# The first norm of a two-layer backbone, made feature block by feature block

## What is computed

```python
sc = jax.nn.silu(c);  sc_ctx = jax.nn.silu(c_ctx)
for i in range(DEPTH):
    sh1, sc1, g1, sh2, sc2, g2 = split(sc @ ada_w[i] + ada_b[i], 6)        # context: the same with sc_ctx
    h  = rmsnorm(x, norm1_w[i]) * (1 + sc1) + sh1                          # rmsnorm: x * rsqrt(mean(x*x) + eps) * w
    hc = rmsnorm(ctx, norm1_w[i]) * (1 + csc1) + csh1
    y, yc = retention(h, hc, ...) if i % 2 == 0 else neighbourhood_attention(h, hc, ...)
    x = x + g1 * y;  x = x + g2 * conv_ffn(rmsnorm(x, norm2_w[i]) * (1 + sc2) + sh2)
    ...                                                                     # the context likewise, in layer 0
return rmsnorm(x, final_norm_w)

# retention: q, k, v, g = split(h @ w_in); axial rope on latent q, k; forward and backward decay per head;
# out = (silu(g) * rmsnorm_per_head(o)) @ w_out
```

## Time and profile before

| what | us |
|---|---|
| median of 3 runs | 2104.57 |
| the runs | 2098.45, 2104.57, 2106.68 |
| the profiled execution's own time | 2100.11 |
| its span in the trace | 2098.2 |
| TensorE busy in it | 1994.6 |
| VectorE busy | 1336.1 |
| ScalarE busy | 749.5 |

### The profile page before, as it was taken

How to read it: one execution, slowest core, us unless ns; L and a number is a source line. 1 busy time by engine, 2 the same in 40 slices (tenths; PEclk the granted TensorE clock), 3 DMA queues, 4 the chain that set the end, 5 groups by cost and what they waited for, 6 DMA issues and landing times.

```text
span 2098.2 us, 30012 instructions
## 1 busy us (share of the span) xinstructions
PE 1994.6 (95%) x10500; PEld 1702.0 (81%) x10500; DVE 1336.1 (64%) x2241; ACT 749.5 (36%) x1274; POOL 97.4 (5%) x162
## 2 busy tenths in 40 slices
PE   5989999999999989999999999799999789999997
PEld 5778888888888868888888888688888668888885
DVE  5665735635745677766664567777877557557476
ACT  3333223313313343412331233456556335324242
POOL 0000000000000000000000000211111000000000
PEclk9999999999999989999999999899999899999998
DMA  7221221221221112233224324211111212222222
GB/s 278 71 90 61 100 71 61 82 91 61 79 93 61 61 41 100 92 128 120 90 90 132 108 95 152 102 46 41 55 45 35 81 61 100 100 97 93 97 93 101
DMA packets 50762, 186.40 MB, mean 89 GB/s; under 512 B 5569, under 2 KB 5569, under 8 KB 50561
## 3 DMA queue, kind: packets, MB, share of 16 engines
q1 hardware_dynamic: 37248, 136.73, 18.9%
q0 software_dynamic: 13440, 48.63, 6.9%
HBM read 181.15 MB, written 4.19 MB: 88 GB/s over the span
## 4 chain that ended last, share of the span: by engine, by line
PE 84%; DVE 7%; issue 4%; ACT 3%; DMA 1%; DVEq 0%; SPq 0%; ACTq 0%
PE acc L383 58%; PE o_ps L469 4%; PE o_ps L500 3%; PE acc L469 3%; PE acc L588 3%; PE o_ps L631 2%; PE acc L646 2%; PE acc L487 2%; PE acc L434 2%; PE o_ps L646 2%; DVE pt_lo L1548 1%; DMA x<-in_x_in_dram 1%; PE acc L621 1%; PE o_ps L420 1%; ACT w_hi L779 1%
## 5 line engine op out<-in xcount | busy, mean ns | idle before, releaser
L779 ACT ACTIVATE w_hi<-raw 128x1024 fp32r<-128x1024 f32 x232 | 245.1, 1057 | 615.3 <-PE acc L383 498.2
L1125 DVE TENSOR_TENSOR w_lo<-raw,w_hi 128x1024 fp32r<-128x1024 f32 x232 | 284.0, 1224 | 272.6 <-ACT w_hi L779 271.1
L383 PE MATMUL acc<-h_hi,w_hi 128*128 128x512 f32 x1520 | 434.6, 349 | 4.6 <-DVE w_lo L1125 3.4
L383 PE MATMUL acc<-h_lo,w_hi 128*128 128x512 f32 x1520 | 434.4, 349 | 0.0
L383 PE MATMUL acc<-h_hi,w_lo 128*128 128x512 f32 x1520 | 434.3, 349 | 0.0
L383 PEld LDWEIGHTS acc<-h_hi,w_hi 128*128 128x128 f32 x1520 | 244.0, 188 | 45.7 <-ACT u L942 4.2
L383 PEld LDWEIGHTS acc<-h_hi,w_lo 128*128 128x128 f32 x1520 | 243.9, 188 | 39.3
L383 PEld LDWEIGHTS acc<-h_lo,w_hi 128*128 128x128 f32 x1520 | 243.2, 188 | 38.9
L1253 DVE SCALAR_TENSOR_TENSOR x<-acc,mod,x 128x512 f32<-128x512 f32 (+3 forms) x136 | 81.9, 636 | 144.9 <-PE acc L383 136.0
L383 PE MATMUL acc<-act_hi,w_lo 128*128 128x512 f32 (+1 forms) x396 | 119.7, 356 | 0.0
L383 PE MATMUL acc<-act_lo,w_hi 128*128 128x512 f32 (+1 forms) x396 | 119.6, 356 | 0.0
(11 more groups left out here) (224 smaller groups left out, 3536.9 us busy)
## 6 DMA issues: line engine op xcount, KB each, us to landing
raw<-in_weights_dram SPq DMA_DIRECT2D x232, 512.0 KB, 3.3
ada_raw<-in_ada_dram POOLq DMA_DIRECT2D x80, 512.0 KB, 3.5
ada_start<-in_ada_first_dram SPq DMA_DIRECT2D x4, 2048.0 KB, 22.4
x<-in_x_in_dram SPq DMA_DIRECT2D x1, 3072.0 KB, 23.5
park_dram<-x POOLq DMA_DIRECT2D x1, 2048.0 KB, 8.1
rel<-in_bias_dram POOLq DMA_DIRECT2D x16, 128.0 KB, 2.4
out_dram<-x SPq DMA_DIRECT2D x8, 256.0 KB, 2.1
x<-park_dram POOLq DMA_DIRECT2D x1, 1536.0 KB, 9.1
```

The source lines that it names most:

```text
L383: mm = nc.tensor.matmul(tile[:, c0:c0 + cn], wt[:, b * P:(b + 1) * P], mv[:, n, c0:c0 + cn], start=(n == 0 and m == 0), stop=(n == last an ...
L779: nc.scalar.activation(w_hi[i][:, :], raw[i][:, :], ACT.Copy).then_inc(hi_split, 1)
L1125: nc.vector.tensor_tensor(w_lo[i][:, :], raw[i][:, :], w_hi[i][:, :].bitcast(F32), ALU.subtract)\
```

## The change

- `x` is loaded right behind the constants, in 4 pieces of two feature blocks, each with a semaphore of its own; `squares` waits for each piece. The rows of conditioning come behind it.
- The modulation weights come in 8 pieces of 1 MB, one for each feature block: its scale weights for DVE and its shift weights, laid out for TensorE in blocks 1, 2, 4, 6, 7 (`PE_SHIFTS`) and for DVE in blocks 0, 3, 5. The two first weight chunks stand between them. POOL's first `ada_raw` waits until the last scale row is made.
- TensorE makes `token_sums` and `spread_roots` first, then the shift rows of blocks 1 and 2, and those of 4, 6 and 7 between the values' products of blocks 1 and 2, 3 and 4, and 4 and 5.
- ACT copies the spread roots to `ss`. DVE goes block by block: the scale row, the shift row (its own, or one small addition to TensorE's), `x * root` in one instruction for all tokens, then `h_lo` of the block before. ACT makes `x * root * a + shift` in float32 and then `h_hi`, so `h_lo` is a plain difference.
- In head 0 the decay tables and the first later row (`ada_step(0)`) stand ahead of the keys instead of behind them, and ACT's gate waits until the last query is in halves.

```diff
 PARTS = ((0, LAT, 0), (LAT, CTX, 1))
+PE_SHIFTS = (1, 2, 4, 6, 7)
...
-                ada_start = [sb(f"ada_start{i}", [P, 4, D], stack=part) for i in range(4)]
+                ada_start = [sb(f"ada_start{k}", [P, 2, D], stack=part) for k in range(KC)]
...
         spread = o_ps[:, 0:2, :].rearrange("p a t -> p (a t)")
+        shifts = [o_ps[:, n % 2, 2 * n:2 * n + 2] for n in range(len(PE_SHIFTS))]
...
             sp.dma_start(small[:, :], small_in).then_inc(const_in, 16)
+            for i in range(4):
+                sp.dma_start(x[:, 2 * i:2 * i + 2, :], x_in[:, 2 * i:2 * i + 2, :]).then_inc(x_loaded[i], 16)
             for c in range(2):
                 sp.dma_start(silu_rows[:, c, :], cond_rows[c, :].partition_broadcast(P)).then_inc(rows_in, 16)
-            for i in (2, 0, 1, 3):
-                if i == 1:
-                    sp.dma_start(x[:, :, :], x_in).then_inc(x_loaded, 16)
-                sp.dma_start(ada_start[i][:, :, :], ada_first[4 * i:4 * i + 4, :, :].rearrange("a p n -> p a n"))\
-                  .then_inc(ada_start_in[i], 16)
-            sp.dma_start(raw[0][:, :], weights[0, :, :]).then_inc(raw_in[0], 16)
-            sp.dma_start(raw[1][:, :], weights[1, :, :]).then_inc(raw_in[1], 16)
+            for k in range(KC):
+                sp.dma_start(ada_start[k][:, :, :], ada_first[2 * k:2 * k + 2, :, :].rearrange("a p n -> p a n"))\
+                  .then_inc(ada_start_in[k], 16)
+                if k in (0, 2):
+                    sp.dma_start(raw[k // 2][:, :], weights[k // 2, :, :]).then_inc(raw_in[k // 2], 16)
...
         def _(pool):
-            pool.dma_start(ada_raw[:, :], ada[0, :, :]).then_inc(ada_in, 16)
             nc.gpsimd.memset(ones[:, :], 1.0).then_inc(set_up, 1)
             nc.gpsimd.iota(dist[:, :], pattern=[[1, 896]], base=-384, channel_multiplier=-1,
                            allow_small_or_imprecise_dtypes=True).then_inc(set_up, 1)
+            pool.wait_ge(start_rows, 1)
+            pool.dma_start(ada_raw[:, :], ada[0, :, :]).then_inc(ada_in, 16)
...
+            def start():
+                pe.wait_ge(set_up, 1)
+                token_sums(KC, TOK)
                 spread_roots(PARTS)
+                pe.wait_ge(cond_done, 1)
+                shift_row(1)
+                shift_row(2)
+            def shift_row(k):
+                n = PE_SHIFTS.index(k)
+                pe.wait_ge(ada_start_in[k], 16)
+                if n == 0:
+                    pe.wait_ge(spread_copied, 1)
+                elif n > 1:
+                    pe.wait_ge(shift_taken, n - 1)
+                for j in range(KC):
+                    mm = nc.tensor.matmul(shifts[n], ada_start[k][:, 1, j * P:(j + 1) * P], silu_c[:, j, :],
+                                          start=(j == 0), stop=(j == KC - 1))
+                mm.then_inc(shift_made, 1)
...
                                 mm.then_inc(full, 1)
+                        if first and k == 4:
+                            shift_row(PE_SHIFTS[4])
                     if s < 3:
                         mm.then_inc(v_used, 1)
+                    if first and s < 2:
+                        shift_row(PE_SHIFTS[2 + s])
...
                 return i, after
-            def squares(src, n, width):
+            def squares(src, n, width, loaded=None):
                 for k in range(n):
+                    if loaded is not None and k % 2 == 0:
+                        act.wait_ge(loaded[k // 2], 16)
...
+            def start_norm():
+                act.wait_ge(spread_done, 1)
+                nc.scalar.activation(ss[:, :], spread[:, 0:TOK], ACT.Copy).then_inc(spread_copied, 1)
+                nc.scalar.activation(logs[:, :, 0:2], cols["dlog"].rearrange("p (h c) -> p h c", c=2), ACT.Exp)\
+                  .then_inc(logs_done, 1)
+                split()
+                for k in range(KC):
+                    act.wait_ge(norm_t, normed.up())
+                    if k >= 2:
+                        act.wait_ge(h_lo_done, k - 1)
+                    for c0, cn, c in PARTS:
+                        ins = nc.scalar.activation(S[k % 2][:, c0:c0 + cn], S[2 + k % 2][:, c0:c0 + cn], ACT.Identity,
+                                                   scale=norm_a[:, k, c:c + 1], bias=mod[:, 0, k, c:c + 1])
+                    ins.then_inc(h_made, 1)
+                    act.wait_ge(h_made, k + 1)
+                    nc.scalar.activation(h_hi[:, k, :], S[k % 2][:, 0:TOK], ACT.Copy).then_inc(h_hi_done, 1)
+                    if k == 1:
+                        split()
+                    elif k in (3, 5, 7):
+                        value_split()
...
             def head_front(first):
                 if first:
-                    value_split()
-                    value_split()
                     take_values(True)
                     split()
+                    decay_tables()
                 for j in range(4):
                     key_hi(j)
+                if not first:
+                    decay_tables()
+                    for _ in range(OUT_SLOTS):
+                        wait_full()
+                        wait_full()
+                        split()
...
                 if first:
+                    act.wait_ge(qk_lo_done, 4)
                     gate(0, *wait_at(0))
...
             act.wait_ge(const_in, 16)
             nc.scalar.activation(silu_c[:, :, :], cond, ACT.Silu).then_inc(cond_done, 1)
-            nc.scalar.activation(logs[:, :, 0:2], cols["dlog"].rearrange("p (h c) -> p h c", c=2), ACT.Exp)\
-              .then_inc(cond_done, 1)
+            squares(x, KC, TOK, x_loaded)
             act.wait_ge(rows_in, 32)
-            nc.scalar.activation(silu_rows[:, :, :], silu_rows[:, :, :], ACT.Silu).then_inc(cond_done, 1)
-            A.next_at(1, counted=False)
-            act.wait_ge(x_loaded, 16)
-            squares(x, KC, TOK)
+            nc.scalar.activation(silu_rows[:, :, :], silu_rows[:, :, :], ACT.Silu).then_inc(rows_done, 1)
             act.wait_ge(set_up, 1)
             root(D, TOK)
-            for _ in range(2):
-                split()
-            norm(0, 0, PARTS, rooted=True, between=value_split)
+            start_norm()
...
+            def start_norm():
+                own_shift = lambda k: mod[:, 0, k, :]
+                def row(k, r, made):
+                    place = ada_start[k][:, r, :]
+                    step(nc.vector.tensor_tensor_reduce(ada_raw[:, :], place, silu_rows[:, 1, :], 1.0, 0.0, ALU.mult,
+                                                        ALU.add, mod_new[:, made, 1:2]))
                     step(nc.vector.tensor_tensor_reduce(place, place, silu_rows[:, 0, :], 1.0, 0.0, ALU.mult, ALU.add,
+                                                        mod_new[:, made, 0:1]))
+                def scale(k):
+                    dve.wait_ge(ada_start_in[k], 16)
+                    row(k, 0, k)
+                    made = nc.vector.tensor_scalar(norm_a[:, k, :], mod_new[:, k, :], lift[:, k:k + 1], norm_w[:, 0, k:k + 1],
+                                                   ALU.add, ALU.mult)
+                    if k == KC - 1:
+                        made.then_inc(start_rows, 1)
+                def shift(k):
+                    if k in PE_SHIFTS:
+                        n = PE_SHIFTS.index(k)
+                        dve.wait_ge(shift_made, n + 1)
+                        nc.vector.tensor_scalar(own_shift(k), shifts[n], ada_b[:, 0, k:k + 1], None, ALU.add)\
+                          .then_inc(shift_taken, 1)
+                    else:
+                        made = (k + KC // 2) % KC
+                        row(k, 1, made)
+                        nc.vector.tensor_scalar(own_shift(k), mod_new[:, made, :], ada_b[:, 0, k:k + 1], None, ALU.add)
+                def rooted_x(k):
+                    nc.vector.tensor_tensor(S[2 + k % 2][:, 0:TOK], x[:, k, :], ss[:, :], ALU.mult).then_inc(norm_t, 1)
+                def low(k):
+                    dve.wait_ge(h_hi_done, h_hi_made.up())
+                    nc.vector.tensor_tensor(h_lo[:, k, :], S[k % 2][:, 0:TOK], h_hi[:, k, :].bitcast(F32), ALU.subtract)\
+                      .then_inc(h_lo_done, 1)
+                step(nc.vector.tensor_scalar(lift[:, :], ada_b[:, 0, KC:2 * KC], 1.0, None, ALU.add))
+                add_squares(KC, TOK)
+                dve.wait_ge(rows_done, 1)
+                scale(0)
+                one_over(TOK)
+                shift(0)
+                split()
+                dve.wait_ge(spread_copied, 1)
+                rooted_x(0)
+                for k in range(1, KC):
+                    scale(k)
+                    shift(k)
+                    rooted_x(k)
+                    low(k - 1)
+                    if k in (2, 4, 6):
+                        split()
+                low(KC - 1)
+                split()
+                normed.up(KC)
+                h_split.up(KC)
...
             def head_front(hd, first):
                 if first:
```

(71 more changed lines are left out.)

52 lines of the change are left out of this document (11 added, 41 removed).

## The result

| | us |
|---|---|
| changed kernel, median of 6 runs | 2088.80 (2081.45 to 2089.32) |
| kernel before, 6 runs beside it | 2105.62 (2098.45 to 2107.43) |
| ratio | 0.9918, 95% interval 0.9902 to 0.9933 |
| span of the profiled execution | 2086.8 (before: 2098.2) |

Faster by 0.8%, 16.8 us between the medians; 18.4 were forecast, and a time of 2084.0. The range (2074 to 2092) holds it. The profiled execution of the changed kernel took 2089.09, near the slow end of its six.

A forecast was written before the change was run, and what follows sets the result against it. TensorE's work or idle time was taken as the bound. Start 12.3, head 0 4.9 and clock 1.2 sum to 18.4 off the profiled 2100.11, giving 2081.7; plus 2.3 for the runs, 2084.0 us, range 2074 to 2092.

The forecast's parts named there:

- Transfers: Loads at the start: nearly in issue order, some 0.7 MB late; x complete at 13.8, first modulation piece 18.7.
- Rival (b): Start loads: x's pieces share engines with later transfers, last lands some 12 us later; gain 10.4, 2092; 7%.
- The start: Steps up to the first product on h: it starts at 35.5, 24.0 us before the old 59.49.
- TensorE and T: Values' projection: VectorE paces up to block 4, TensorE is the bound after; first key product at 81.7, 12.3 earlier.
- T: Start time of the first key product: 94.0 before, forecast 81.7, bounds 79.4 and 86.5.
- Rival (a): Values' projection and head: every pause costs clock, T = 86.5, no clock gain in head; gain 12.4, 2090; 20%.
- rival (d): Values' projection: the clock never rises, T = 107; 8 us slower overall, 2110; 4%.
- Head 0: First attention head: values' product starts 4.9 us earlier relative to T, leaving 2.5 of 7.42 idle.
- the 4.9: Head 0: us gained before the values' product by earlier decay tables, with the gate's new wait covering the table load.
- the 1.2: Head 0: us counted for an even chance that the clock holds through 2.5 idle, which would save 2.7.
- Rival (c): Head 0 gives nothing because another wait fills the hole; gain 12.3, 2090; 6%.
- The sum: Whole kernel: 12.3 + 4.9 + 1.2 = 18.4 us gained, forecast time 2084.0.

The follow-up runs named there:

- a0: The changed kernel unchanged, measured again beside two variants: median 2084.72 us, ratio to the kernel before 0.9911.
- e5: Changed kernel with head 0's decay tables behind the queries again and no extra gate wait: head's values' product 52.56 us behind T.
- e6: Changed kernel plus a one-element silu ahead of the gate's waits, loading the table there: head's values' product 47.64 us behind T.
- e3: Changed kernel with all eight shift rows on VectorE, none on TensorE: T 93.62, one run 2102.9 us.
- e7: Changed kernel with the previous block's h_lo made right behind the scale row, before shift row and x * root: T 78.44.
- e2: Kernel before, with x loaded behind the constants in 4 pieces, all else unchanged: T 98.47, one run 2111.5 us beside 2101.7.
- e4: Changed kernel with TensorE's shift rows of blocks 4, 6 and 7 made twice, same result: T 83.34.
- e9: The e8 version with block 3's shift row on TensorE too: median 2078.55 us, ratio to the kernel before 0.9867.
- e8: Changed kernel with both the e6 and e7 edits: median 2083.11 us, ratio to the kernel before 0.9899.
- e1: Changed kernel with x loaded in one transfer at the same place in the queue: T 85.14.

## Why the prediction was right, step by step

- **Transfers.** The last square's sum was forecast for 16.6 and came at 15.3, the rows' silu for 16.3 and came at 14.97, the first modulation piece for 18.7 and came at 17.6. The rows and that piece landed when 4.89 and 5.96 MB had moved, 0.3 MB behind their turn and not 0.7. The sum's step was read a little wrong: it was tied to the last piece of `x` (forecast for 13.8), but that landed at about 11.8, and from 10.99 on ScalarE waited for VectorE's eight sums and not for a transfer. Rival (b) is out: the last piece of `x` came 2 sooner than forecast and not some 12 later.
- **The start.** First product forecast 35.5, measured 34.73. VectorE's blocks, forecast at 4.5 and 7.05, took 4.59 and 7.13 (`h_lo` of block 0 begun at 33.72, of 4 at 59.43).
- **TensorE and T.** Forecast 81.7, measured 81.71, and 80.56 in a0. That it fits to the hundredth is luck, since the parts were off and cancelled: block 4 began 0.7 earlier than forecast (60.44 and not 61.1), took 7.2 with its restart at half level and not 6.3, and the row of block 7 took 1.68 and not 2.0. One fall of the clock on the path, at block 4, was the right count, and e5, e6 and a0 had it too. In a0 and e6 the level fell in block 2 as well, which VectorE's pace covered, as the prediction had said of that place. Rival (a) is out, since T is not 86.5 in any of the four and only block 4's fall stood on the path; rival (d) is out, since the level rose within every block where it had fallen.
- **Head 0.** The term that was sized wrong is the 4.9: I wrote that the new wait "covers the table load". It measured 3.64 (e5), because the load starts behind both waits (124.18, when the product ended at 124.12), and e6 gives back 1.28 by moving it. So the 2.5 of idle were 3.8, and the clock fell. Of the 1.2 counted there 0.9 came, by luck: the 1.2 stood for an even chance at no fall, and what came is a shorter stretch at half level, which e3 and e7 did not have behind the same idle time. Rival (c) is out by e5.
- **The sum.** To the end of head 0's values the changed kernel is 16.9 ahead (155.72 against 172.58 for the context's products), against 18.4 forecast; of what is missing some 1.3 is the table load and 0.3 the clock. Between the medians it was 16.8 as well, but that the two agree is partly luck: the profiled pair ends only 11.4 apart, and a0's rounds gave 19.5. The forecast time of 2084.0 stood 4.8 below the measured median. 1.6 of that is the gain; the other 3.2 come from where I placed the runs, 2.3 above the profile's 2100.11, when the median of the six is 5.5 above it.

The profiled pair shows only 11.4 between the spans. The lead is kept through layer 0 and shrinks in layer 1, as these rows show, first of the kernel before and then of the changed one: the sums ahead of layer 1 and the last sums.

```profile
1313.57 2.72 PE L413 MATMUL o_ps<-ones,ss 128*128 128x2 f32 x12 [3.51 <-DVE ss L1151]
...
2085.72 1.05 PE L413 MATMUL o_ps<-ones,ss 128*128 128x2 f32 x8 [2.28 <-DVE ss L1151]
```
```profile
1296.38 2.72 PE L424 MATMUL o_ps<-ones,ss 128*128 128x2 f32 x12 [3.51 <-DVE ss L1182]
...
2074.44 1.05 PE L424 MATMUL o_ps<-ones,ss 128*128 128x2 f32 x8 [2.28 <-DVE ss L1182]
```

The changed kernel is 17.2 ahead when layer 1 begins and 11.3 at its end. Part is the clock around the norm ahead of the last FFN, before and now:

```profile
1707.70:1745.00 37.30, 31.54 (x125) 24.59 (x126) 26.26 (x45) 17.25 (x26) 0.00 (x0) 0.86 0.18 60
```
```profile
1691.30:1728.60 37.30, 31.51 (x111) 24.38 (x112) 23.42 (x42) 16.07 (x24) 0.00 (x0) 0.77 0.18 57
```

14 fewer products in the same 37.3, at 0.77 of the clock and not 0.86. Across this stretch the lead goes from 16.4 (the sums, at 1707.75 and 1691.37) to 14.8 (the FFN's first product, at 1729.74 and 1714.92). Another 3.5 lie in the last FFN, 359.5 against 356.0. 1.6 of them are in its first group (84.8 against 83.2), which differs among runs of either version: e2 has the longer, e5 the shorter. Behind it TensorE is at full granted clock. Between the same two waits, 576 products each:

```profile
1813.00:1944.80 131.80, 131.28 (x576) 108.05 (x576) 78.51 (x104) 42.39 (x64) 0.00 (x0) 1.00 0.28 96
```
```profile
1799.80:1932.30 132.50, 132.08 (x576) 107.97 (x576) 78.53 (x104) 42.39 (x64) 0.00 (x0) 1.00 0.29 95
```

The changed kernel takes 0.7 longer here and 1.2 from there to the last sums (142.1 against 140.9), 1.9 us in all. It goes with the program and not with the run: between these two waits the kernel before and e2, a version of it, take 131.9, and all ten profiles of the changed kernel and its variants 132.6. It can go the other way too: the longest run of products in layer 0's FFN, 1056 of them, takes 184.0 in those two and 183.5 in all the others. The cause was not found.

## What to carry to other kernels

When a start is a chain through several engines, first move off it the work that stands ahead of a short step and is not needed by it (TensorE's shift rows before the sums); an earlier transfer alone can make it slower (e2). When a consumer needs one block at a time, make each block's share just ahead of it and balance the shares over the engines, and in such a loop finish the block before as soon as its input is there, not behind the next block's rows. A function table is loaded where the instruction stands behind its waits; a one-element call ahead of the waits hides it (e6).

## What the runs showed of the hardware

- A shift row, 8 small products in 16 records, takes 1.68 at full level and 3.48 at half (6.96 for the two at 25.55 in the changed kernel), where I had 2.0 from another shape.
- Small products do not hold the level either. In e4 and e9 the two first rows take 4.73 and 4.79, between the 3.4 of full level and the 6.96 of half, and the granted clock falls at 28.0, in the midst of them, with TensorE busy since 25.5. Of e4 (the granted clock is the third number from the end):

```profile
25.00:27.00 2.00, 1.46 (x14) 1.49 (x14) 0.00 (x0) 1.97 (x4) 0.00 (x0) 1.00 1.03 410
28.00:38.00 10.00, 5.54 (x20) 4.81 (x20) 9.86 (x17) 5.25 (x7) 0.00 (x0) 0.50 1.03 410
```

- The same gap goes either way. The clock held through 2.5 us without work in e6 and e8 (3.01 and 3.00 for 12 products) and fell in e9 through 2.51 (4.49). Ahead of the same products, 3.79 idle gave 4.57 in the changed kernel and in a0, 4.58 in e1, 5.46 in e3, 5.38 in e7, and 2.97, no fall, in e4.
- The level can fall after the work has come back. In the changed kernel the first three steps between the products behind that gap are 0.22 to 0.31, as at full level, and only then they go to 0.43.
- The granted clock of the profile reads 1.00 from 34 to 40 in the changed kernel, while its wide products there start 0.43 apart, against 0.227 behind 39.5; before the first change of level on record it says nothing.
